# Attention scores in three passes over high and low parts of queries and keys, with two roots and one table load placed earlier

## The reference

```
q = concat([q_nope, rope(q_rope)]) * QK_DIM**-0.5          # 64 + 32 = 96 columns a head
k = concat([k_nope, broadcast(rope(kr))])                  # 96 columns a head
s = einsum('bqhd,bkhd->bhqk', qblk, k)                     # fp32
p = softmax(s, axis=-1)
o = einsum('bhqk,bkhd->bqhd', p, v)
```

## Time and profile before

| what | before |
|---|---|
| time, median of 3 runs | 1469.53 us (1469.01 to 1471.03) |
| time of the profiled execution | 1469.52 us |
| its span | 1467.7 us |
| granted TensorE clock, mean | 0.998 |
| PE busy | 1446.0 us (99%), 7072 matmul records |
| PEld busy | 1183.7 us (81%) |
| DVE, ACT, POOL busy | 819.1, 548.1, 661.4 us |

### The profile page before, as it was taken

The page is one execution under the profiler, slowest core; times in us unless marked ns, Lnnn a source line. Parts: engine busy times, 40 slices in busy tenths (PEclk is TensorE's granted clock), DMA queues, the critical chain, the costliest instruction groups (busy, mean ns, idle before and its releaser), DMA issues.

```text
span 1467.7 us, 19031 instructions
## 1 busy us (share of the span) xinstructions
PE 1446.0 (99%) x7072; PEld 1183.7 (81%) x7072; DVE 819.1 (56%) x1110; ACT 548.1 (37%) x1025; POOL 661.4 (45%) x531
## 2 busy tenths in 40 slices
PE   7999999999999999999999999999999999999998
PEld 5888888878757777888888888888888888888886
DVE  6135555454676776166783865455455655446465
ACT  6223323234245555345323433332223333244452
POOL 4374536266100002455565664545444454454481
PEclk9999999999999999999999999999999999999999
DMA  5221111112240002534533311111111113623252
GB/s 201 65 65 36 29 40 25 26 25 68 53 100 1 1 1 101 173 93 144 175 128 100 94 58 58 51 51 49 37 59 58 51 58 127 210 87 123 87 156 96
DMA packets 91724, 115.94 MB, mean 79 GB/s; under 512 B 13680, under 2 KB 54640, under 8 KB 91120
## 3 DMA queue, kind: packets, MB, share of 16 engines
q1 hardware_dynamic: 91632, 114.72, 25.7%
HBM read 102.11 MB, written 10.49 MB: 77 GB/s over the span
## 4 chain that ended last, share of the span: by engine, by line
PE 92%; DVE 3%; issue 2%; ACT 1%; POOL 1%; DMA 0%; SPq 0%; DVEq 0%; POOLq 0%; ACTq 0%
PE ps L50 24%; PE ps L52 24%; PE ps L51 24%; PE ps L1546 4%; PE ps L1564 4%; PE ps L912 4%; PE ps L1554 2%; PE ps L1005 1%; PE ps L1401 1%; PE ps L959 1%; PE ps L944 1%; PE ps L956 0%; DVE total L1985 0%; PE ps L1000 0%; PE ps L1002 0%
## 5 line engine op out<-in xcount | busy, mean ns | idle before, releaser
L1314 POOL TENSOR_TENSOR wy_low<-w_raw,wy_high 128x512 fp32r<-128x512 f32 x230 | 330.4, 1437 | 362.4 <-ACT wy_high L1295 362.0
L1295 ACT ACTIVATE wy_high<-w_raw 128x512 fp32r<-128x512 f32 x230 | 145.0, 631 | 392.9 <-PE ps L52 388.0
L50 PE MATMUL ps<-wy_high,hid_high 128*128 128x512 f32 x512 | 199.4, 389 | 0.4 <-DVE hid_low L1889 0.4
L51 PE MATMUL ps<-wy_low,hid_high 128*128 128x512 f32 x512 | 199.2, 389 | 0.0
L52 PE MATMUL ps<-wy_high,hid_low 128*128 128x512 f32 x512 | 199.2, 389 | 0.0
L1975 DVE TENSOR_TENSOR total<-total,ps 128x512 f32<-128x512 f32 x184 | 124.8, 686 | 101.4 <-PE ps L52 101.4
L363 POOL TENSOR_TENSOR wx_low<-w_raw,wx_high 128x512 fp32r<-128x512 f32 (+1 forms) x64 | 85.0, 1335 | 144.0 <-ACT wx_high L464 144.0
L50 PE MATMUL ps<-a_high,wy_high 128*128 128x512 f32 x352 | 137.5, 391 | 0.0
L52 PE MATMUL ps<-a_high,wy_low 128*128 128x512 f32 x352 | 137.0, 389 | 0.0
L51 PE MATMUL ps<-a_low,wy_high 128*128 128x512 f32 x352 | 137.0, 389 | 0.0
L50 PEld LDWEIGHTS ps<-wy_high,hid_high 128*128 128x128 f32 x512 | 96.1, 188 | 20.7 <-issue 0.6
(11 more groups left out here) (235 smaller groups left out, 2989.0 us busy)
## 6 DMA issues: line engine op xcount, KB each, us to landing
w_raw<-in_w_up SPq DMA_DIRECT2D x88, 256.0 KB, 2.8
w_raw<-in_w_down SPq DMA_DIRECT2D x88, 256.0 KB, 2.6
w_raw<-in_w_in SPq DMA_DIRECT2D x62, 256.0 KB, 2.8
w_raw<-in_w_o SPq DMA_DIRECT2D x32, 256.0 KB, 2.6
w_raw<-in_w_ple_gate SPq DMA_DIRECT2D x32, 256.0 KB, 2.6
x_tile<-in_x SPq DMA_DIRECT2D x8, 512.0 KB, 7.3
x_res<-in_x SPq DMA_DIRECT2D x8, 512.0 KB, 5.4
keep_x<-x_res SPq DMA_DIRECT2D x8, 512.0 KB, 4.0
```

Source lines behind the costliest of these rows:

```text
L50: pe.matmul(out, stat_high, mov_high, start=start, stop=False)
L51: pe.matmul(out, stat_high, mov_low, start=False, stop=False)
L1295: act.activation(out, tile_raw(tile), ACT.Copy).then_inc(high_made, 1)
L1314: pool.tensor_tensor(low_tile, tile_raw(tile), high_tile.bitcast(F32), ALU.subtract).then_inc(low_made, 1)
```

## The change

Queries and keys of the attention are split into high and low parts while the loop runs. The first eight steps (tile 0) keep the plain F32 matmul; from the ninth on the scores go through `three_passes`. There are 30 parts: the keys of 8 heads for each sequence, and of each query tile from tile 1 on two halves of 4 heads, each part 96 x 512. ACT copies the high part, POOL subtracts; the low part takes the place of the operand itself. `score_parts` gives the step in which a part is issued. The high keys of the first sequence lie where `a_low` of tiles 0 to 3 is written, so turn and split of these tiles are moved to tiles 4 to 7. Three parts of `hgrn_norm` move to other steps. In the front, root 3 and root 4 stand ahead of the low parts of the first two weight tiles, mean 3 ahead of scale 2, and DVE's four operations of the lower bounds behind the last `low_of`. A small exponential is issued on ACT behind the copy of value tile 5, ahead of the copy of tile 7, which makes its table be loaded there.

```
+        q_high = at("q_high", [QK, 2, 4, P], F32R, a_at + 28672)
+        q_low = at("q_low", [QK, AH, T], F32R, hid_at)          # where q_t lies
+        k_low = at("k_low", [QK, AH, T], F32R, x_at)            # where k_t4 lies
...
 pool_front:
                 root(2)
+                root(3)
                 low(0)
-                root(3)
+                root(4)
                 low(1)
-                for t in range(4, TT):
+                for t in range(5, TT):
...
 act_front (behind the copy of v_att[:, m, :]):
+                        if m == 5:
+                            act.activation(lb_exp[:, 0:1], minus_half[:, 0:1], ACT.Exp)
 dve_front:
                 low_of(0)
+                mean_of(3)
                 scale(2)
-                mean_of(3)
                 low_of(1)
-                (the four operations lb_inv, lb_soft, lb, lb_rest)
                 scale(3)
...
                     if t < 6:
                         scale(t + 2)
+                (the four operations lb_inv, lb_soft, lb, lb_rest)
 back_of:
+            def score_parts(step):
+                t, h = step // AH, step % AH
+                parts = []
+                if 1 <= step <= AH:
+                    parts.append(("k", 0, step - 1))
+                if h == 5 and t < TT - 1:
+                    parts.append(("q", t + 1, 0))
+                if h == 1 and 1 <= t < TT:
+                    parts.append(("q", t, 1))
+                if 1 <= t < QT and h in (4, 6, 7) and 3 * (t - 1) + (4, 6, 7).index(h) < AH:
+                    parts.append(("k", 1, 3 * (t - 1) + (4, 6, 7).index(h)))
+                return parts
+            def score_high(act, part):
+                raw, high_part, _ = score_slices(part)
+                kind, one, two = part
+                if kind == "q" and one >= 2:
+                    act.wait_ge(s_full, (one - 1) * AH + 4 * two + 4)
+                else:
+                    act.wait_ge(s_full, 2)
+                act.activation(high_part, raw, ACT.Copy).then_inc(score_high_made, 1)
+            def score_low(pool, part):
+                raw, high_part, low_part_of = score_slices(part)
+                pool.wait_ge(score_high_made, score_at[part] + 1)
+                if part[0] == "k" and part[1] == 0:
+                    pool.wait_ge(s_full, part[2] + 1)
+                pool.tensor_tensor(low_part_of, raw, high_part.bitcast(F32), ALU.subtract).then_inc(score_split, 1)
 act_attention:
-                    if h == 4 and 2 <= t < 6:
-                        turned(act, 0, t - 2)
+                    if h == 4 and 4 <= t < 8:
+                        turned(act, 0, t - 4)
+                    for part in score_parts(s):
+                        score_high(act, part)
 pool_attention (roots at h == 3 and h == 4 of a loop over the steps):
+                    for part in score_parts(s):
+                        score_low(pool, part)
 dve_attention:
-                        if h in (3, 4, 6):
-                            hgrn_norm(t, (3, 4, 6).index(h))
+                        if h in (3, 6):
+                            hgrn_norm(t, h // 6)
                         if t and h == 4:
                             norm_mean(t - 1)
-                        if 2 <= t < 6 and h in (5, 7):
-                            low_half(dve, 0, t - 2, h // 7)
+                            hgrn_norm(t - 1, 3)
+                        if 4 <= t < 8 and h in (5, 7):
+                            low_half(dve, 0, t - 4, h // 7)
                     if t and h == 0:
-                        hgrn_norm(t - 1, 3)
+                        hgrn_norm(t - 1, 2)
+                        if t == TT:
+                            hgrn_norm(t - 1, 3)
 pe_attention:
+                        if t == 0:
+                            pe.matmul(ps[:, s % 2, :], q_t[:, h, 0:P], k_t4[:, h, 0:SEQ], start=True, stop=True).then_inc(s_full, 1)
+                        else:
+                            q_part, k_part = ("q", t, h // 4), ("k", t // QT, h)
+                            pe.wait_ge(score_split, max(score_at[q_part], score_at[k_part]) + 1)
+                            three_passes(pe, ps[:, s % 2, :], q_high[:, h // 4, h % 4, :], q_low[:, h, t * P:(t + 1) * P],
+                                         k_high[t // QT][h][:, :], k_low[:, h, t // QT * SEQ:(t // QT + 1) * SEQ],
+                                         True, True).then_inc(s_full, 1)
-                    if h == 3 and 2 <= t < 6:
-                        turn(pe, 0, t - 2)
+                    if h == 3 and 4 <= t < 8:
+                        turn(pe, 0, t - 4)
```

More of the change, by code:

```diff
@@ L101, in trunk_kernel @@
         stat_at = a_at + 65536
+        q_high = at("q_high", [QK, 2, 4, P], F32R, a_at + 28672)
+        q_low = at("q_low", [QK, AH, T], F32R, hid_at)
+        k_low = at("k_low", [QK, AH, T], F32R, x_at)
+        spare_at = [pair_at_byte, pair_at_byte + 2048, wy_low_at, wy_low_at + 2048, pair_at_byte + 6144, pair_at_byte + 4096,
+                    wy_low_at + 4096, stat_at + 1536]
+        k_high = [[at(f"k_high{g}_{h}", [QK, SEQ], F32R, a_at + 32768 + 2048 * h if g == 0 else spare_at[h])
+                   for h in range(AH)] for g in range(2)]
         assert stat_at + 2048 <= x_at
@@ L1230, in back_of, with score_slices @@
                                         for i, n in enumerate(("hg_ssq", "hg_mean", "hg_rstd")))
+            def score_parts(step):
[10 more added lines that the diff above has]
+                return parts
+            score_at = {part: n for n, part in enumerate(part for step in range(STEPS) for part in score_parts(step))}
+            def score_slices(part):
+                kind, one, two = part
+                if kind == "q":
+                    here = (slice(None), slice(4 * two, 4 * two + 4), slice(one * P, (one + 1) * P))
+                    return q_t[here], q_high[:, two, :, :], q_low[here]
+                here = (slice(None), two, slice(one * SEQ, (one + 1) * SEQ))
+                return k_t4[here], k_high[one][two][:, :], k_low[here]
             att_out = hg_vg[:, 0, :, :]
@@ L1545, in pe_attention @@
                             pe.wait_ge(p_made, s - 1)
-                        pe.matmul(ps[:, s % 2, :], q_t[:, h, t * P:(t + 1) * P],
-                                  k_t4[:, h, t // QT * SEQ:(t // QT + 1) * SEQ], start=True, stop=True).then_inc(s_full, 1)
+                        if t == 0:
[6 more added lines that the diff above has]
+                                         True, True).then_inc(s_full, 1)
                     if 1 <= s <= STEPS:
```

30 lines of the change are left out of this document (17 added, 13 removed).

## The result

The changed kernel takes 1460.93 us (median of 4 runs, 1459.22 to 1462.61) against 1470.28 us for the kernel before on the same chip. The ratio is 0.9937 with a 95% interval of 0.992 to 0.9954, so it is 9.3 us faster, give or take 2.5. The forecast was 1461.3. The profiled execution took 1461.89 us with a span of 1460.1, 7.6 us less than the profiled one of before.

A forecast was written before the change was run, and what follows sets the result against it. TensorE was taken to bound the kernel. From 1469.52 us, the attention's -7.5 (-8.4 + 0.6 + 0.3), the front's -0.7 and the table's 0 gave 1461.3 us; 8-in-10 range 1456.5 to 1465.8.

The forecast's parts named there:

- The scores: Attention, 56 of 64 steps: three passes replace the F32 score matmul, 0.15 us saved a step, 8.4 us.
- rival A: Attention scores: the first pass hides its extra cost, 12.1 us gained in all, 1457.4 us; chance 0.13.
- The loop: Attention, scores through DVE and ACT back to PE's transposes: keeps up, slack falls from 0.28 to 0.14 us.
- POOL and DVE: Attention: POOL's subtractions delay DVE's HGRN products; 0.3 us lost, bounds 0 and 7.8 us.
- Rival B: Attention: POOL's subtractions hold DVE's products beyond the slack; 1469 us, or 1465.2 with half of them; chance 0.18.
- The table: Attention's start: loading the exponential's table earlier gains at most 0.04 us, put at 0.
- The front: Kernel's start: roots set forward close two PE idle gaps of 0.18 and 0.52 us, together 0.7 us gained.
- The second gap: Front: PE's 0.52 us idle up to 22.16, waiting for low_of 3, closes with root 4 set forward.
- The sum: Whole kernel: 1469.52 less 7.5 for the attention, 0.7 for the front, 0 for the table: 1461.3 us.
- the long step: Attention, step 61: turned tile meets the next stage's first weight tile's high part on ACT; 0.6 us lost once.

The follow-up runs named there:

- e5: Changed kernel without the pass of high queries and low keys, parts still made: 1452.68 us, ratio 0.9880 to the kernel before.
- e6: Changed kernel with only the pass of high queries and high keys, parts still made: 1446.94 us, ratio 0.9843 to the kernel before.
- e1: Kernel before with only the front's edits: 1470.35 us, ratio 1.0001 to the kernel before.
- e9: e5 also without POOL's 16 subtractions for the keys' low parts: 1451.54 us, ratio 0.9875 to the kernel before.
- e2: Kernel before with only the attention's edits, front and table load as before: 1461.61 us, ratio 0.9945 to the kernel before.
- e12: e3 run once more, the same code: 1461.44 us, ratio 0.9944 to the kernel before.
- e3: Changed kernel with tile 2's first weight chunk product repeated twice in TensorE's idle gap in the front: 1460.92 us, ratio 0.9938 to the kernel before.

## Why the prediction was right

**The scores.** Right in mechanism and size. 0.78 for three passes was read off a place where they follow short matmuls, and the first pass paid 0.32 there as here. The step shrank by 0.164 instead of 0.15, mostly because the values' pitch is 0.03 shorter, while F32 to three passes gave 0.13: 56 x 0.164 = 9.2. The plain pitch of 0.23 (rival A) would have given 3 us too much. That an F32 matmul's two records are "one for each of its passes" is a reading of the records; what the runs show is the price, 0.91 against 0.78.

**The loop.** The slack was real and small: 0.12 to 0.26 us measured against 0.14. The one loss that was forecast, where the turned tile meets the first weight tile on ACT, came in the step named, 0.34 and 0.05 us instead of 0.6. No other changed step was longer than PE's own work. e5 and e6 show how close that was. The second path over ACT's copy was not in the forecast.

**POOL and DVE.** DVE's product stands still as the row had it (1221 ns on average), and by the times forecast: the one at 475.48 ends 2.87 us into its step, where 2.9 was expected. It cost PE nothing in the full change, where 0.3 had been allowed. Rival B, priced at 3.9 to 7.8 us, failed on its condition: the product sits in even steps that have room for 0.6 us more.

**The table.** Right: nothing to gain from a load that was hidden behind a maximum.

**The front.** This is the step that failed: "The second gap closes too. Together 0.7 us." DVE moved as worked out and the turn of tile 4 came 0.8 us earlier in the profile. In the changed kernel's profile the gap did not close: with fast products ahead of it PE was done at 19.57 instead of 21.46 and waited longer, and behind the wait the clock fell and cost 1.65 us up to the next turn. The forecast took PE's work in the front at the speed of the one trace at hand, whose products had the pitch of the lower level up to about 20 us, and it did not name that as a condition. Where the new front's first products were slow too (e1, e5, e6, e9), the turn of tile 5 came 0.67 us sooner, as forecast. The runs give the front's part as 1.0001 (0.9992 to 1.0010): no gain, though 0.7 us lies inside the interval.

**The sum** was right partly because two errors cancelled: the attention gave 8.8 us and not 7.5, the front 0 and not 0.7. The attention's 1.3 us are 0.8 from the passes (9.2 for 8.4), 0.2 from the long step (0.39 for 0.6) and 0.3 that was allowed for POOL and DVE and not needed. By the medians the gain is 9.3 +- 2.5, and the profiles' 7.6 includes a front in which the clock fell.

## What to carry to other kernels

Where one engine is full, price a cheaper instruction by the start-to-start pitch at a place with the same neighbours, not by its pitch in a long run of its kind; then add up the loop that returns to that engine, because its slack shrinks twice, by the step and by the instruction. Before setting a small thing forward (a table load, a root), look at what starts last behind it: the table load ended 0.02 us before the maximum did, and was worth nothing. A gain in a start-up phase should be read in several executions, since the clock can be at either level there and can turn the gain into a loss; say for which level the forecast is worked out.

## What was not expected of the hardware

**The rise.** The first products of the same instructions ran at the pitch of 2.4 GHz from 16 us in some executions, and in others at that of 1.2 GHz up to 18 to 20 us. After an early rise and 1.8 us of idle PE the 2 us stretches behind it read 0.50 to 0.65 in each of five cases. After an early rise and 1.75 us of idle PE in the old front (e2) they read 1.00.

**A fall without idle time.** In every one of the 14 profiles the clock also falls between 334 and 340 us, in the recurrence, with PE busy before and behind the fall. The fall comes during or just behind 32 products with a single column each. The rows are the kernel before, and the stretch of 11 us in it and in e1:

```profile
334.27 3.63 PE L968 MATMUL ps<-ones,latent_sq 128*128 128x1 f32 x32
```

```profile
334.00:345.00 11.00, 11.00 (x67) 10.30 (x67) 3.31 (x7) 3.98 (x7) 5.65 (x6) 0.84 0.19 48
334.00:345.00 11.00, 11.00 (x51) 10.13 (x51) 3.30 (x7) 2.30 (x4) 4.63 (x5) 0.69 0.25 63
```

From the first of these products to the eighth weight product behind them it took 11.75 to 11.79 us in ten executions, and 13.37 to 13.41 in four (e1, e5, e9, e12), in which the low stretch was longer. A busy PE in the profile is thus no promise of a full clock. Whether the single columns are the cause was not tried.

**The scatter of a time.** The 31 runs of the kernel before took 1468.6 us on average with a mean granted clock of 0.999 (4 runs), 1469.6 with 0.998 (16) and 1471.2 with 0.997 (11). So much of the difference between runs of one kernel goes with the clock. Single waits add to it: in the change, e2 and e3 PE waits twice for 0.55 us behind DVE's scores, in none of the other eleven; and a wait for a weight tile near 328 us is 1.04 or 1.05 us in nine profiles, 0.49 in four and absent in e1. From the turn of tile 5 to the first score, where PE's code is the same in all, the profiles took 400.7 (e6) to 403.5 us (e12). This is why the attention's 8.8 us are taken between its own landmarks.
